# Narrower token tiles for small experts, and a coarser ladder of widths above 128, in a one-core MoE layer

## The reference, cut to what matters

```python
logits = (h @ router_w + router_b).astype(jnp.float32)
top_vals, top_idx = lax.top_k(logits, TOP_K)      # 4 of 32 experts per token
...
gate = jnp.minimum(xb @ w_gate[e] + b_gate[e], SWIGLU_LIMIT)
up = jnp.clip(xb @ w_up[e] + b_up[e], -SWIGLU_LIMIT, SWIGLU_LIMIT)
act = gate * jax.nn.sigmoid(SWIGLU_ALPHA * gate) * (up + 1.0)
y = act @ w_down[e] + b_down[e]
```

## Time and profile before

| | before |
|---|---|
| three executions | 2072.0, 2073.2, 2074.21 us |
| median | 2073.2 us |
| the profiled execution's span | 2073.2 us |
| TensorE busy | 2011.8 us, 97% of it |
| the experts, first to last group | 514 to 2055 us |

### The profile page before, as it was taken

The page is one execution under the profiler, slowest core; times in us unless marked ns, Lnnn a source line. Parts: engine busy times, 40 slices in busy tenths (PEclk is TensorE's granted clock), DMA queues, the critical chain, the costliest instruction groups (busy, mean ns, idle before and its releaser), DMA issues.

```text
span 2073.2 us, 32125 instructions
## 1 busy us (share of the span) xinstructions
PE 2011.8 (97%) x13457; PEld 1643.8 (79%) x13458; DVE 655.5 (32%) x1363; ACT 283.8 (14%) x457; POOL 232.9 (11%) x381
## 2 busy tenths in 40 slices
PE   8999988996999999999999999999999999999996
PEld 4444455554998898889788999988888888989996
DVE  3115676443223222222222332222222222222223
ACT  2001245111011001101001010111010100100103
POOL 0001333212000001000001010010000000000103
PEclk9999999997999999999999999999999999999998
DMA  4210022214878879998999988899899998887855
GB/s 173 81 41 1 1 92 84 100 61 152 305 248 305 307 272 322 321 329 296 321 322 318 309 294 272 286 319 335 312 304 322 319 319 310 279 299 260 287 189 199
DMA packets 231449, 500.89 MB, mean 242 GB/s; under 512 B 7766, under 2 KB 8303, under 8 KB 231298
## 3 DMA queue, kind: packets, MB, share of 16 engines
q1 hardware_dynamic: 218880, 454.46, 61.0%
q0 software_dynamic: 12368, 44.26, 8.6%
q10 hardware_dynamic: 50, 0.01, 0.0%
HBM read 463.63 MB, written 35.13 MB: 241 GB/s over the span
## 4 chain that ended last, share of the span: by engine, by line
PE 72%; DMA 1%; DVE 1%; issue 1%; SPq 0%; ACT 0%; POOL 0%; POOLq 0%; DVEq 0%; ACTq 0%
PE ps L1694 57%; PE ps L1721 12%; PE ps L1708 2%; PE ps L1714 1%; PE ps L1701 1%; DMA qk<-x_rows 1%; DMA out<-qk 0%; DVE x L1254 0%; DMA hT<-h_rows,hT 0%; DMA x_rows<-x,hT 0%; DVE qk L1363 0%; SPq L439 0%; DVE xn L1221 0%; ACT hT L821 0%; ACT x L857 0%
## 5 line engine op out<-in xcount | busy, mean ns | idle before, releaser
L1694 PE MATMUL ps<-hT,qk 128*128 128x128 f32 (+8 forms) x4096 | 501.7, 284 | 6.8 <-issue 6.8
L1694 PEld LDWEIGHTS ps<-hT,qk 128*128 128x128 f32 x4096 | 493.5, 192 | 16.6 <-issue 16.0
L1721 PE MATMUL ps<-w_ring,hT 128*128 128x512 f32 x576 | 251.8, 593 | 0.0
L1694 PE MATMUL ps<-hT,u_all 128*128 128x128 f32 (+8 forms) x2048 | 247.7, 282 | 0.0
L1694 PE MATMUL ps<-hT,v 128*128 128x128 f32 (+8 forms) x2048 | 247.7, 282 | 0.0
L1694 PEld LDWEIGHTS ps<-hT,v 128*128 128x128 f32 x2048 | 244.6, 191 | 0.0
L1694 PEld LDWEIGHTS ps<-hT,u_all 128*128 128x128 f32 x2048 | 244.6, 191 | 0.0
L1694 PE MATMUL ps<-hT,w_ring 128*128 128x132 f32 (+7 forms) x1792 | 233.8, 291 | 5.0 <-DVE x L1254 3.6
L1694 PEld LDWEIGHTS ps<-hT,w_ring 128*128 128x128 f32 x1792 | 229.3, 190 | 7.4 <-issue 7.0
L1721 PEld LDWEIGHTS ps<-w_ring,hT 128*128 128x128 f32 x576 | 107.5, 190 | 126.7 <-issue 126.3
L558 POOL DMA_INDIRECT hT<-h_rows,hT x46 | 45.3, 986 | 1148.9 <-issue 672.1
(11 more groups left out here) (250 smaller groups left out, 1470.6 us busy)
## 6 DMA issues: line engine op xcount, KB each, us to landing
w_ring<-in_w_down SPq DMA_DIRECT2D x64, 2048.0 KB, 7.9
qk<-in_w_gate SPq DMA_DIRECT2D x32, 2048.0 KB
qk<-in_w_up SPq DMA_DIRECT2D x32, 2048.0 KB
v<-in_w_gate SPq DMA_DIRECT2D x32, 2048.0 KB, 10.5
u_all<-in_w_up SPq DMA_DIRECT2D x32, 2048.0 KB, 8.7
x<-in_b_down SPq DMA_DIRECT2D x32, 512.0 KB, 11.6
w_ring<-in_w_in SPq DMA_DIRECT2D x3, 2048.0 KB, 9.0
x<-in_x SPq DMA_DIRECT2D x8, 512.0 KB, 12.4
```

Source lines behind the costliest of these rows:

```text
L1694: ins = pe.matmul(bank[:, m, 0:n], w[g][:, k, m * P:(m + 1) * P], rhs[:, k, 0:n], start=k == 0, stop=k == KC - 1)
L1721: ins = pe.matmul(ps[:, 2 * (g % PAIRS), :], aT[:, k, 0:P], w[g][:, k, :], start=k == 0, stop=k == KC - 1)
```

## The change

The ladder of widths gets three steps below 128 and loses three above it: 132, 140 and 148 go (136, 144 and 152 stay or take their place). `ONE_BLOCK` is the index of 128, and each place that asked whether the index is above 0 now asks whether it is above `ONE_BLOCK`. With the token counts above, three experts go from 128 columns to 96 (2, 17, 22), three to 108 (5, 10, 21), six to 120 (7, 9, 12, 18, 19, 25), and six stay at 128. Experts 0 and 13 go from 132 to 136, experts 8 and 29 from 140 to 144; the other ten above 128 keep their width. Down of a one-block expert still runs on 128 rows.

```diff
-WIDTHS = (128, 132, 136, 140, 144, 148, 152, 160, 168, 180, 192)
+WIDTHS = (96, 108, 120, 128, 136, 144, 152, 160, 168, 180, 192)
+ONE_BLOCK = WIDTHS.index(P)
...
         def past_first(eng, wide, body):
 
-            with eng.If(wide > 0):
+            with eng.If(wide > ONE_BLOCK):
                 body(2)
...
                 def expert(i, n):
                     e = nc.snap(e_reg, min_val=0, max_val=E - 1)
+                    two_blocks = i > ONE_BLOCK
...
-                    if i:
+                    if two_blocks:
                         product(4, aT, early)
                     else:
                         rows_of(4, range(KC // 2))
...
-                    with pe.If(after > 0):
+                    with pe.If(after > ONE_BLOCK):
                         with pe.If(after > len(WIDTHS) - 1):
                             call(hints, after, len(WIDTHS), len(WIDTHS))
                         with pe.Else():
                             pe.wait_ge(xT_ready, 2 * e + 3)
                             pe.sem_inc(passed, 1)
                             turn_in(1).then_inc(turn_mm[1], 1)
-                            call(hints, after, 1, len(WIDTHS) - 1)
+                            call(hints, after, ONE_BLOCK + 1, len(WIDTHS) - 1)
...
                     with pe.Else():
                         pe.sem_inc(turn_mm[1], 1)
-                        call(hints, after, 0, 0)
+                        call(hints, after, 0, ONE_BLOCK)
                     ready(5)
-                    (product(5, aT) if i else rows_of(5, range(KC))).then_inc(group_done, 1)
-                    pe.reg_mov(before, int(i > 0))
+                    (product(5, aT) if two_blocks else rows_of(5, range(KC))).then_inc(group_done, 1)
+                    pe.reg_mov(before, int(two_blocks))
```

More of the change, by code:

```diff
@@ L832, in back @@
                     wide = width_of(act, e)
-                    with act.If(wide > 0):
+                    with act.If(wide > ONE_BLOCK):
                         for h, n in enumerate(HALVES):
@@ L1724, in turn_second @@
                 def turn_second(e, wide):
-                    with pe.If(wide > 0):
+                    with pe.If(wide > ONE_BLOCK):
                         pe.wait_ge(xT_ready, 2 * e + 1)
@@ L1822, in expert @@
                     pe.sem_inc(passed, 1)
-                    (product(4, aT, late) if i else rows_of(4, range(KC // 2, KC))).then_inc(group_done, 1)
+                    (product(4, aT, late) if two_blocks else rows_of(4, range(KC // 2, KC))).then_inc(group_done, 1)
                     hints = {}
-                    with pe.If(after > 0):
+                    with pe.If(after > ONE_BLOCK):
                         with pe.If(after > len(WIDTHS) - 1):
@@ L1866, in _ @@
                 nc.switch_bb("experts_end", parent=start)
-                with pe.If(width_of(pe, E - 1) > 0):
+                with pe.If(width_of(pe, E - 1) > ONE_BLOCK):
                     pe.wait_ge(y_ready, 2 * E)
```

## The result

Before 2073.2 us (2072.0 to 2074.2, 5 runs), changed 2080.7 us (2077.5 to 2081.9, 5 runs): ratio 1.0033, 95% interval 1.0021 to 1.0046. The change makes the kernel slower. The profiled execution of the changed kernel has a span of 2079.0 us and a time of 2080.7: 1.7 us lie around the span, and 1.7 to 2.0 us in the other runs where both are known. The span of before equals the median only by chance: by this reckoning its profile (span 2073.2) belongs to an execution some 2 us above the median, and the two spans are only 5.8 us apart. From the start of the first group 0 to the end of the last group 5 the experts take 6.8 us longer, and 5.6 us in a second profile (e9).

A forecast was written before the change was run, and what follows sets the result against it. TensorE was taken as one unbroken chain, with the weight load setting the pace at 128 columns and below. Terms -0.2 + 5.1 + 0.4 + 1.4 = +6.7 us on 2073.2 gave 2079.9 us, range 2073.5 to 2085.

The forecast's parts named there:

- Narrow tiles: Gate and up of the 12 narrower experts: group price unchanged at 7.14 us, gain 0.2 us, between 0 and 1.
- Wide tiles: Experts 0 and 13 at 136 columns, 8 and 29 at 144: 1.3 us each, 5.1 us of loss.
- Among wide bodies: Jumps between wide bodies: tree levels as before for most, stops stay within 0.2 us, counted as nothing.
- The way to the first body: Before expert 0: three more comparisons in the open cost 0.4 us; the fetch stays at 6.1 us.
- Handovers from wide to one-block bodies: Before experts 9 and 21 stops grow 0.4 us each; 0.1 us at six places: 1.4 us, from 0 to 6.
- From one-block bodies: Jumps behind one-block experts: 7.5 us of queued matmuls cover tree and comparisons, so no cost.
- the first, that columns count below 128: Rival on gate and up: columns set the time below 128 too, giving 2036 to 2048 us; chance 7%.
- The second, a first fetch that goes away: Rival before expert 0: the 6.1 us fetch is spared, giving 2073.8 us, no difference; chance 16%.
- The third, waits at jumps to other code: Rival at ten jumps between one-block experts: fetches outlast their cover, 2090 to 2136 us; chance 5%.

The follow-up runs named there:

- e9: The changed kernel, word for word, run and profiled again: 2080.7 us, ratio 1.0039.
- e5: The kernel before, with gate and up of all 18 one-block experts moving 96 columns: 2071.9 us, ratio 0.9996.
- e1: The changed kernel with widths 132, 140 and 148 put back, so only the three steps below 128 are new: 2074.3 us, ratio 1.0006.
- e8: The changed kernel with an extra width of 64 that no expert uses, so every body lies one further back: 2076.5 us, ratio 1.0017.
- e10: The kernel before without any prefetch hints, one execution: 2131.2 us.
- e12: The kernel before, tree and hint moved between the parts of group 4 in wide bodies, ahead of the transposes in one-block bodies: 2072.8 us, ratio 1.0000.
- e6: The kernel before, with gate and up of the one-block experts moving 64 columns, one execution: 2076.7 us.
- e4: The kernel before, with the tree of comparisons and its hint ahead of group 4 instead of group 5: 2084.3 us, ratio 1.0054.

## Why the prediction was right

The forecast was 2079.9 us, measured were 2080.7, in the range and slower as forecast. Term by term, from the distances between the experts' starts in the profiles of before and after:

- **Narrow tiles, 0.2 us of gain.** The mechanism is shown: 7.12 to 7.14 us a group at 96 to 120 columns, and e5 with nothing else changed. The gain is 0.5 to 0.6 us.
- **Wide tiles, 5.1 us.** Right: groups 7.42 and 7.84 us, and the distance that expert 29 takes grew by 1.2.
- **Among wide bodies, nothing.** Mis-sized. I counted the levels of the tree and found them alike for most; the standstills before group 5 of experts 0, 13, 14 and 15 went from 0.85, 0.83, 0.78 and 0.75 us to 0.45, 0.28, 0.36 and 0.33, and with three smaller ones 2.1 us came back. About 1 us of it is in experts 13 and 15, where a level went. In experts 0 and 14 the way to the hint has as many levels as before; in expert 14 the same four comparisons got shorter, and they did so with the old tree as well (e1). Nor had VectorE long been done there, as the prediction has it: in expert 13 of the kernel before it ended 0.5 us before group 5 began.
- **The way to the first body, 0.4 us.** 6.29 us against 6.09, and 5.55 in e9: the three comparisons do not show above what differs from run to run.
- **Handovers from wide to one-block bodies, 1.4 us.** The step that failed in its detail. I had both existing stops grow by 0.4 us because the hint comes later. It does not come later as seen from the jump: 6.9 us ahead for 7.0 before expert 21. And with the same lead that jump takes 3.77 us here, 0.37 in e1 and 0.39 in e8. Instead of growing, the stop before expert 9 vanished, the one before expert 21 grew from 0.50 to 2.40 us, and one of 1.22 us appeared before expert 1, between two wide bodies, where I had put nothing. And I had no term for what a standstill does to the clock: 1.7 us after the one before expert 21. Together 1.22 + 2.40 + 1.7 - 0.76 = 4.6 us. It stayed within the bound of 6 us that I had given the handovers.
- **From one-block bodies, nothing.** Right: ten changes of body, seven of them with jumps of 2.2 to 3.97 us, and no standstill. That hints matter for this cover is shown by e10 for the jumps to wide bodies: four of six took 6.1 to 6.8 us without them.

So -0.5 + 5.1 - 2.1 + 0.2 + 4.6 = 7.3 us for 6.7, where the experts' distances and the first stop give 6.8 + 0.2 = 7.0. The sum was closer than its parts, as a loss and a gain that I had missed nearly offset each other. That the forecast came within 1 us is in good part luck: the same matmuls with every body one place further back (e8) take 2076.5 us. What was right with its reason is the floor, the price of the wide tiles and the cover behind one-block bodies.

Of the rivals, the first, that columns count below 128, fell with e5. The weight-load floor of the Trainium skill ("TensorE: Matmul & The Clock Gate", section "LDWEIGHTS (loading the stationary operand)") has the right form; its 106.7 ns are 111.6 here. The second, a first fetch that goes away, did not happen in any kernel. The third, waits at jumps to other code, is real: it struck at seven of the ten narrow jumps, under queued matmuls that covered it, and behind wide bodies, where they did not. The Trainium skill, "Runtime: NRT & Kernel Launch", section "Instruction fetch mechanics", has such stalls for taken branches to code out of reach, without a duration. That the length of these waits depends on where bodies lie is shown by e8 and e9 together, with the same bodies in use and the hint as far ahead of the jump. It cannot be the place alone: from the body of 108 to that of 128 the jump takes 2.64 us before expert 6 and 0.23 before expert 11 of one execution, and 2.67 and 0.23 in e9. Perhaps what ran before counts too, which is not shown. Which boundary in the code's memory makes a jump long was not tried.

## What to carry to other kernels

Fewer moving columns help only while the columns and not the weight loads set the pace: compare a wide and a narrow matmul start to start before cutting tiles, here 7.14 us a group from 96 to 128 columns. Where code branches between large bodies, look at the comparison that jumps and at how much work is queued under it; adding or removing a body moves the waits of all the others, so that a change of a few us in such a kernel should be repeated with the bodies shifted. A stop of over 2 us in a full TensorE can cost more than itself, since the clock may fall behind it; here that was 1.7 us more.

## What the runs showed of the hardware that was not expected

- With 32 moving columns under weight loads at full pace, the clock fell to 1.2 GHz inside the experts although the profile shows TensorE busy throughout, and the kernel took 2515.6 us; with 64 it fell once and with 96 never.
- A standstill of 2.40 us (and one of 2.61 us in e12) was followed by 3.4 us at 1.2 GHz; those of up to 1.84 us were not, but for the one in e6, and neither was that of 3.16 us in e4. Of the nine of 2.06 to 3.34 us at the starts of experts in e10, seven came with such a fall, those of 2.24 and 2.52 us did not. What decides it stays open.
- A prefetch hint 4 to 9 us ahead of the jump served most jumps, but given 13 to 16 us ahead (e4, e12) it left 2.6 to 3.7 us for the same two jumps that took about 0.4 before, to experts 1 and 17. The other jumps behind wide bodies had as early a hint there and took 0.2 to 0.4 us. Without hints, most jumps to another body took 3.3 to 7.9 us.
- One comparison of the same tree, on the same way through it, took 0.48 us in one kernel, and none took more than 0.21 in another (expert 14, before and e1).
